# A pooled half copied between two heads' exponentials, and copies and scales ahead of two weight splits

## The reference, cut to what matters

```python
h = u @ w_in_pool[j]
tok = pool_mixer(h[..., :TOK_WIDTH], w_pool_group[j], pool_scale[j])
qm = h[..., TOK_WIDTH:]
mo = mem_cross_attention(qm, mem_n, w_mem_kv[i], mem_q_gain[i], mem_k_gain[i])
x = x + jnp.concatenate([tok, mo], axis=-1) @ w_out[i]
u = rms_norm(x, g_mlp[i])
x = x + jnp.square(jax.nn.relu(u @ w_ff1[i])) @ w_ff2[i]
```

## Time and profile before

| what | value |
|---|---|
| median of the runs shown | 810.45 us (809.8 to 810.87, 3 runs) |
| profiled execution, own time | 810.04 us |
| its span | 808.2 us |
| PE busy | 797.9 us, 99% |
| DVE busy | 537.1 us, 66% |
| ACT busy | 416.1 us, 51% |
| chain that ended last, share of PE | 89% |
| mean granted clock | 0.999 |

### The profile page before, as it was taken

The page is one execution under the profiler, slowest core; times in us unless marked ns, Lnnn a source line. Parts: engine busy times, 40 slices in busy tenths (PEclk is TensorE's granted clock), DMA queues, the critical chain, the costliest instruction groups (busy, mean ns, idle before and its releaser), DMA issues.

```text
span 808.2 us, 11167 instructions
## 1 busy us (share of the span) xinstructions
PE 797.9 (99%) x4190; PEld 662.9 (82%) x4190; DVE 537.1 (66%) x728; ACT 416.1 (51%) x589; POOL 110.3 (14%) x143
## 2 busy tenths in 40 slices
PE   8999999999999999999999999999999999999998
PEld 6998977778878777888888888887777888888886
DVE  5647988767585767566665566578875666665561
ACT  5646656554655554365444435448654545444440
POOL 1610300000020510030000000067920000000000
PEclk9999999999999999999999999999999999999999
DMA  8961444345736633646655556461324466655541
GB/s 312 322 197 41 157 157 157 117 160 215 253 135 233 212 120 105 208 141 201 218 174 202 185 182 204 157 208 53 118 91 157 157 213 222 204 191 202 168 149 53
DMA packets 76742, 140.43 MB, mean 174 GB/s; under 512 B 2936, under 2 KB 23104, under 8 KB 76704
## 3 DMA queue, kind: packets, MB, share of 16 engines
q1 hardware_dynamic: 74608, 134.03, 49.3%
q0 software_dynamic: 1936, 5.82, 2.2%
q10 hardware_dynamic: 160, 0.07, 0.0%
HBM read 138.86 MB, written 1.05 MB: 173 GB/s over the span
## 4 chain that ended last, share of the span: by engine, by line
PE 89%; DVE 5%; ACT 2%; DMA 2%; issue 1%; SPq 0%; POOL 0%; DVEq 0%; ACTq 0%
PE bank L1744 57%; PE bank L2123 13%; PE bank L2125 7%; PE bank L1910 2%; PE bank L2127 2%; DVE w_lo L1184 2%; PE bank L1825 2%; PE bank L1971 1%; PE bank L1878 1%; PE bank L1945 1%; DMA raw<-in_w_in 1%; DVE prob L1356 1%; PE bank L1758 1%; DMA raw<-in_w_mem_kv 1%; PE bank L1951 0%
## 5 line engine op out<-in xcount | busy, mean ns | idle before, releaser
L1744 PE MATMUL bank<-w_hi,a_both 128*128 128x512 f32 (+2 forms) x752 | 234.5, 383 | 0.5 <-PE bank L1744 0.4
L1184 DVE TENSOR_TENSOR w_lo<-raw,w_hi 128x2048 fp32r<-128x2048 f32 (+2 forms) x65 | 146.2, 2250 | 51.8 <-ACT w_hi L727 51.4
L1627 DVE TENSOR_TENSOR w_lo<-raw,w_hi 128x2048 fp32r<-128x2048 f32 x48 | 110.0, 2292 | 91.5 <-ACT w_hi L1087 90.5
L2123 PE MATMUL bank<-a_both,w_hi 128*128 128x512 f32 x448 | 161.4, 399 | 0.0
L1744 PEld LDWEIGHTS bank<-w_hi,a_both 128*128 128x128 f32 x752 | 140.7, 188 | 22.9 <-issue 1.9
L1087 ACT ACTIVATE w_hi<-raw 128x2048 fp32r<-128x2048 f32 x48 | 92.0, 1917 | 111.9 <-PE bank L1744 53.4
L1744 PE MATMUL bank<-w_hi,b_hi 128*128 128x512 f32 x376 | 148.9, 396 | 0.1
L727 ACT ACTIVATE w_hi<-raw 128x2048 fp32r<-128x2048 f32 (+1 forms) x63 | 119.1, 1893 | 56.4 <-PE bank L1744 34.3
L1744 PE MATMUL bank<-w_lo,b_hi 128*128 128x512 f32 x376 | 146.5, 390 | 0.0
L1744 PE MATMUL bank<-w_hi,b_lo 128*128 128x512 f32 x376 | 146.5, 390 | 0.0
L1744 PE MATMUL bank<-w_lo,a_both 128*128 128x512 f32 (+2 forms) x376 | 141.7, 377 | 0.0
(11 more groups left out here) (244 smaller groups left out, 855.3 us busy)
## 6 DMA issues: line engine op xcount, KB each, us to landing
raw<-in_w_ff SPq DMA_DIRECT2D x64, 1024.0 KB, 5.2
raw<-in_w_in_moba SPq DMA_DIRECT2D x20, 512.0 KB, 4.2
raw<-in_w_merge SPq DMA_DIRECT2D x8, 1024.0 KB, 5.1
raw<-in_w_out SPq DMA_DIRECT2D x8, 1024.0 KB, 5.1
m<-in_w_in SPq DMA_DIRECT2D x6, 880.0 KB, 8.8
raw<-in_w_mem_kv SPq DMA_DIRECT2D x4, 1024.0 KB, 5.2
raw<-in_w_ple_gate SPq DMA_DIRECT2D x4, 1024.0 KB, 5.0
raw<-in_w_in_pool SPq DMA_DIRECT2D x4, 1024.0 KB, 5.1
```

The source lines that it names most:

```text
L1184: dve.tensor_tensor(w_lo[:, v % RING, 0:n], landing[land_slot(v)][:, 0:n], w_hi[:, v % RING, 0:n].bitcast(F32), ALU.subtract).then_inc(lo_ ...
L1627: dve.tensor_tensor(w_lo[:, (base + c) % RING, :], raw[:, (base + c) % RAW, :], w_hi[:, (base + c) % RING, :].bitcast(F32), ALU.subtract). ...
L1744: ins = pe.matmul(banks[t][:, 0:n], xa[:, kt, ts], wa[:, slot, w], start=first and k == 0 and q == 0, stop=last and k == kts - 1 and q == 2)
L2123: pe.matmul(b_hid[f][:, :].rearrange("p (q n) -> p q n", q=2), w_hi[:, slot, w], both_, start=kt == 0, stop=False)
```

## The change

On ACT the exponentials of `second` are issued one head at a time, with `copy_d(0)` between the two heads, and the split of O2 goes from ahead of `out_hi(first)` to behind `copy_pt(second)`. On DVE the split of O1 goes from ahead of `copy_d(1)` to behind `scale_mixed(0)`, and the split of O2 from ahead of `scale_mixed(0)` to behind `group(G_TOK0 + 2)`, at the end of the stage. No instruction is added or removed, and PE's, SP's and POOL's programs stay as they are.

```diff
--- before.py, ACT
             copy_pt(first)
-            exps(second)
+            exps(second, (0,))
             copy_d(0)
-            unit(U_POOL + 3)
+            exps(second, (1,))
             out_hi(first)
             copy_d(1)
             copy_pt(second)
+            unit(U_POOL + 3)
             group(G_TOK0, b_hi, 0)
--- before.py, DVE
             copy_d(0)
             normalise(second)
-            unit(U_POOL + 2)
             copy_d(1)
             copy_pt(second)
             out_lo(first)
-            unit(U_POOL + 3)
             dve.wait_ge(pool_landed, 16 * 7)
             scale_mixed(0)
+            unit(U_POOL + 2)
             group(G_TOK0, b_hi, b_lo, 0)
             scale_mixed(1)
             out_lo(second)
             group(G_TOK0 + 1, b_hi, b_lo, 2)
             group(G_TOK0 + 2, b_hi, b_lo, 4)
+            unit(U_POOL + 3)
             out_projection(U_OUT0, B_OUT0, G_MLP0, GAIN_MLP)
```

## The result

The changed kernel takes 816.35 us (median of 6 runs, 816.05 to 817.05), the kernel before 809.95 beside it (6 runs). The ratio is 1.008, 95% interval 1.007 to 1.0091: the change costs 6.4 us. Run again beside the experiments it took 816.96 against 810.01, ratio 1.0086 (1.0073 to 1.01). The profiled execution took 816.23, its span is 814.4 against 808.2.

What follows compares the result with a forecast made beforehand. PE bounds the kernel, busy 797.9 of 808.2 us, with no gaps in the MLP. Terms -1.0, -0.3, +1.1, +4.9 and +1.5 for the clock give +6.2: from 810.45, forecast 816.6 us, range 814.4 to 818.3.

Steps and rivals of the forecast that it cites:

- Parts 1 and 2: ACT's earlier half copy starts pooled(1) 1.0 us earlier; no DVE split ahead of scale_mixed(0) gains 0.3 at the token group.
- Part 3: O1's split behind scale_mixed(0) issues O3's transfer later, so PE waits 1.1 us ahead of O1's product.
- Part 4: O2's split at the stage's end delays F0's transfer and add_half(0): PE waits 4.9 us ahead of the transposes of x.
- The longer landings: a skill page's 6.15 us for 1 MB, instead of 5.0 to 5.5, would add some 1.5 us over two transfers.
- Part 5: PE's clock falls in or just behind the new wait, costing 1.5 us, the middle of 0.6 and 2.45.
- A sign that had been named against the prediction: the prediction is wrong if the clock stays low for much longer than the wait.
- The wait without the clock: rival: waits as forecast, but the clock stays up or costs under 0.5: +4.7, 815.2 us; chance 0.27.
- A second wait: rival: F1 lands late and PE waits again ahead of the MLP: 818.6 us; chance 0.07.
- a gain that stays: rival: both transfers hide, PE arrives 1.3 us early at the MLP: 809.2 us; chance 0.03.
- a loss that the MLP takes up: rival: the wait comes but the MLP behind the stage takes it up: 810.5 us; chance 0.03.

Runs made afterwards that it cites:

- second profile: the unmodified changed kernel run and profiled once more beside the experiments: 816.96 against 810.01 us for the kernel before.
- the filled wait: changed kernel with 18 extra matmuls, their result never read, just ahead of PE's wait for x: 814.89 against 810.07 us for the kernel before.
- first half of the sum ahead: changed kernel with add_half(0) ahead of the split of F0 on DVE: 814.35 against 809.88 us for the kernel before.
- O1's split back: changed kernel with DVE's split of O1 in its old place, only O2's at the end: 816.11 against 809.88 us for the kernel before.
- DVE's part alone: kernel before with only DVE's two moved splits, ACT as before: 817.80 against 810.01 us for the kernel before.
- longer wait: changed kernel with one more DVE pass of 2.2 us ahead of F0's split: 818.43 against 810.07 us for the kernel before.

## Why the prediction was right

**Parts 1 and 2 (gain 1.3, measured 1.05).** The steps were right and both sizes a little large. `pooled(1)` followed `values(first)` only 0.07 us before the end of its row, not 0.25 as I had assumed. The wait for DVE's scaling fell from 0.40 to 0.17, by 0.2 and not by 0.3.

**Part 3 (wait 1.1, measured 0.85).** O3's transfer took 4.98 us from issue to ACT's start, at the low end of the 5.0 to 5.5, where I had taken 5.3. That the two errors cancel at O1's product (-0.2 forecast and measured) is luck. The experiment with O1's split in its old place shows the trade: this wait goes and that of the half copy comes back, with nothing gained.

**Part 4 (wait 4.9, measured 4.42 as a gap, 4.7 in PE's position).** Each link came as forecast: F0's transfer issued at 324.40, landed by 329.64, split by DVE from 331.59, the sum from 333.80, PE at 335.13, all with 0.43 us of late arrival in them; without it each is at most 0.24 us earlier than forecast.

The longer landings that the prediction set beside its own, for some 1.5 us more, did not come: the two transfers took 4.98 and 5.24 us. Its bounds for this part, 4.2 to 5.1, are not what its own steps give with both transfers at 5.0 or 5.5 (4.0 to 5.0); 4.49 lies in both. F1's transfer took 6.7 us, where the rows had shown 5.5 at most; PE needed it so much later that nothing waited.

Moving O2's split up by one place took the wait away, and so did moving the sums, with the splits left late. What I had not seen is that the same order stands a second time, in `add_half(1)` behind F2's split. It costs nothing in the changed kernel, where PE is late by then and `add_half(1)` again waits for PE, so the sum was right without it; it came out only when the first was mended.

**Part 5 (clock 1.5, measured 1.62, and 2.5 in the second profile).** That the clock would fall was right, and the filled wait shows the term by itself: 1.6 us (2.1 by the second measurement). The size is in part luck. It was the middle of wide bounds, the fall was expected from the span's end alone, and there it came 2.0 us after PE had stopped, but here 4.6 us after (330.71 to 335.3), when PE had just resumed, and 3.2 us after in the second profile. There the cost of 2.53 us is above the upper bound of 2.45, because the low stretch with PE at work, 5.4 us, was longer than the wait, which the bound had taken for its length. In the first it was 3.4. A sign that had been named against the prediction, a clock that stays low for much longer than the wait, is not met in the first profile (3.4 us against 4.4) but nearly so in the second (6.8 against 4.6). The wait without the clock, one of the rivals, was put at +4.7; the filled wait measured +4.8.

**The sum.** +4.49 of position and 1.62 for the clock is +6.1, +6.2 was forecast, +6.4 is the difference of the medians. The spans of the two profiled executions differ by 6.2, and not by this 6.1 and the 0.43 of late arrival; the missing 0.3 us arise behind 577 us, far behind the change. The forecast of 816.6 started from 810.45; beside the changed kernel the one before took 809.95, and from there the same sum gives 816.15 against the measured 816.35. The ends of the stated range, 814.4 and 818.3, do not follow to the tenth from its terms (810.45 + 4.2 - 0.5 is 814.2, 818.0 + 0.5 is 818.5), which decides nothing here. A second wait, a gain that stays and a loss that the MLP takes up did not happen: the MLP behind the stage runs without a gap again, as in the earlier trace rows.

## What to carry to other kernels

Where a weight pipeline's buffers are freed by the same engine that forms the results, moving a cheap split later moves a transfer later; with two landing buffers the loss appears two units on, in whatever small operation is written behind that unit's late split. Follow the freed buffer to its transfer and read what stands behind that unit's split on each in-order engine before moving anything. If the transfer has to be late, put the operation that PE waits for ahead of the split, and look for every place where the same order stands: here one place gave +4.5 and both gave nothing, where the changed kernel lost 6.4 to 6.9 us. A wait of PE of a few us can cost more than its length: 3.8 us less of it gave back 5.4.

## What the runs showed of the hardware

The clock fell in every kernel where PE waited 2.70 us or more in this stretch, and at no gap of 1.04 us or less; no run has a gap between the two. Read from PE's timeline and the view by stretches of each:

| kernel | PE's wait | from PE's stop to the fall | clock low for | of it with PE at work | cost |
|---|---|---|---|---|---|
| first half of the sum ahead | 2.70 | 2.0 | 3.4 | 2.7 | 1.3 |
| O1's split back | 3.85 | 4.5 | 3.4 | 3.4 | 1.6 |
| changed, first profile | 4.42 | 4.6 | 3.4 | 3.4 | 1.6 |
| changed, second profile | 4.58 | 3.2 | 6.8 | 5.4 | 2.5 |
| DVE's part alone | 4.69 | 2.5 | 6.8 | 4.7 | 2.2 |
| longer wait | 6.62 | 3.4 | 6.8 | 3.6 | 1.7 |

The cost is the time by which the stretch between the same two transposes of x behind the wait is longer than in the kernel before. It is 0.46 to 0.48 of the low time in which PE worked, in all six, and does not follow the length of the wait. Why the clock falls sooner in one execution than in another, of the same program too, stays open. The Trainium skill (TensorE: Matmul & The Clock Gate, HAM oscillation — how this bites in real kernels) names, in its abstract rule, a longer gap as the one to avoid than the 2.70 us that were enough here; the runs decide.

Two transfers of 1 MB issued 2.2 us apart do not take the same time: F0's landed in 5.2 us and F1's in 6.7 (5.4 and 7.3 in the second profile), where those of the kernel before had taken 5.0 to 5.5.
